# A four-layer transformer kernel: VectorE's work of the linear attention in other gaps, the up projections begun in another order, and the last attention's turns taken earlier

## The reference, cut to what matters

```python
# layer 2, one direction (the other one runs over the flipped tokens)
decay = exp(where(mask, b[:, :, :, None] - b[:, :, None], -inf))   # b = cumsum(loga)
attn = einsum('bhid,bhjd,bhijd->bhij', q, k, decay)
o = attn @ v + einsum('bhid,bhde->bhie', q * exp(b), S)
o = rms(o_forward + flip(o_backward)) * g_gla * silu(r)
# layer 3, per query block of 128
q = apply_rope(rms_norm(h @ w_q, g_q)); k = apply_rope(rms_norm(h @ w_k, g_k))
o = softmax(q @ k.T * 128 ** -0.5) @ v
# every layer, behind its mixer
h = norm(h + gate * (o @ w_out)); y = act(modulate(h) @ w_up) @ w_down
```

## Time and profile before

| | us |
|---|---|
| median of 3 runs (lowest to highest) | 4195.52 (4193.74 to 4201.62) |
| profiled execution, its own time | 4201.74 |
| its span | 4199.9 |
| TensorE busy | 4017.6 (96%) |
| VectorE busy | 1745.0 (42%) |
| ScalarE busy | 830.5 (20%) |
| GpSimd busy | 292.7 (7%) |
| mean granted clock of TensorE | 0.984 |

### The profile page before, as it was taken

The page is one execution under the profiler, slowest core; times in us unless marked ns, Lnnn a source line. Parts: engine busy times, 40 slices in busy tenths (PEclk is TensorE's granted clock), DMA queues, the critical chain, the costliest instruction groups (busy, mean ns, idle before and its releaser), DMA issues.

```text
span 4199.9 us, 46273 instructions
## 1 busy us (share of the span) xinstructions
PE 4017.6 (96%) x18592; PEld 2493.8 (59%) x18592; DVE 1745.0 (42%) x3018; ACT 830.5 (20%) x1643; POOL 292.7 (7%) x396
## 2 busy tenths in 40 slices
PE   7999999999999999999999997799999999999999
PEld 6676588744455555458745645645555444658864
DVE  0254523101257566444202016637786014437841
ACT  1266111100122222211102014421100021531000
POOL 1000000000003422400000002200000000000000
PEclk9999999999999999999999998999999999999999
DMA  5255011211112222312313112401111111002222
GB/s 182 92 200 183 20 61 60 72 60 40 44 61 91 71 81 90 121 56 88 106 62 111 40 40 102 157 26 57 54 60 61 55 67 63 11 21 82 90 91 75
DMA packets 201200, 325.65 MB, mean 78 GB/s; under 512 B 4274, under 2 KB 90632, under 8 KB 200864
## 3 DMA queue, kind: packets, MB, share of 16 engines
q1 hardware_dynamic: 195136, 302.00, 21.2%
q0 software_dynamic: 5856, 20.73, 1.6%
HBM read 320.56 MB, written 2.16 MB: 77 GB/s over the span
## 4 chain that ended last, share of the span: by engine, by line
PE 90%; DVE 5%; ACT 3%; issue 1%; DMA 1%; POOL 0%; DVEq 0%; ACTq 0%
PE PS L992 27%; PE PS L1032 25%; PE PS L967 3%; PE PS L1509 3%; PE PS L945 3%; PE PS L1086 3%; PE PS L1523 3%; PE PS L904 2%; PE PS L821 2%; PE PS L1510 1%; PE PS L1670 1%; PE PS L1200 1%; PE PS L1680 1%; PE PS L1169 1%; PE PS L947 1%
## 5 line engine op out<-in xcount | busy, mean ns | idle before, releaser
L992 PE MATMUL PS<-RING,BIG 128*128 128x512 f32 x2352 | 1016.6, 593 | 3.7 <-DVEq L1737 1.6
L992 PEld LDWEIGHTS PS<-RING,BIG 128*128 128x128 f32 x2352 | 445.5, 190 | 556.8 <-issue 551.9
L1032 PE MATMUL PS<-UT,RING 128*128 128x256 f32 (+1 forms) x2432 | 643.4, 412 | 16.2 <-ACT BIG L2546 15.1
L1032 PEld LDWEIGHTS PS<-UT,RING 128*128 128x128 f32 x2432 | 463.5, 191 | 157.7 <-issue 20.5
L1032 PE MATMUL PS<-BIG,RING 128*128 128x256 f32 (+1 forms) x1824 | 487.8, 410 | 1.8 <-DVEq L1757 1.0
L1823 DVE TENSOR_TENSOR RES_TMP<-PS,GATE 128x512 f32<-128x512 f32 x80 | 55.3, 691 | 1019.7 <-PE PS L992 950.7
L1032 PEld LDWEIGHTS PS<-BIG,RING 128*128 128x128 f32 x1824 | 345.9, 190 | 107.9 <-DVEq L1757 3.1
L2529 ACT ACTIVATE UT<-PS,COL 128x128 f32<-128x128 f32 x328 | 118.8, 467 | 136.2 <-PE PS L882 134.3
L967 PE MATMUL PS<-RING,UT 128*128 128x512 f32 x320 | 139.6, 598 | 2.5 <-ACT BIG L2834 0.9
L992 PE MATMUL PS<-RING,UT 128*128 128x512 f32 x320 | 139.2, 593 | 2.0 <-issue 1.2
L1509 PE MATMUL PS<-UT,RING 128*128 128x512 f32 x256 | 132.4, 599 | 4.4 <-issue 3.7
(11 more groups left out here) (407 smaller groups left out, 4804.0 us busy)
## 6 DMA issues: line engine op xcount, KB each, us to landing
RING<-w_mod_dram SPq DMA_DIRECT2D x48, 2048.0 KB, 8.1
RING<-w_ffn_up_dram SPq DMA_DIRECT2D x44, 1024.0 KB, 5.0
RING<-ff_w_dram SPq DMA_DIRECT2D x32, 1024.0 KB, 5.5
RING<-ff_w_dram SPq DMA_DIRECT2D x16, 2048.0 KB, 8.0
RING<-ssm_w_in_dram SPq DMA_DIRECT2D x8, 2048.0 KB, 8.2
RING<-w_ffn_down_dram SPq DMA_DIRECT2D x8, 1536.0 KB, 6.6
RING<-w_ffn_down_dram SPq DMA_DIRECT2D x8, 1280.0 KB, 5.9
RING<-ssm_w_out_dram SPq DMA_DIRECT2D x4, 2048.0 KB, 8.1
```

Of the source, the lines that this page charges most:

```text
L992: m = mm(bank(t), inp[:, kk, t * 128:(t + 1) * 128], w[:, k, :], start=kk == 0, stop=kk == kn - 1)
L1032: m = mm(bank(bank_, n), a[:, k, :], b[:, k, :], start=k == 0, stop=k == 3)
```

## The change

In layer 2's levels, `heads` is split in two, and both parts move from behind the even step into the next odd step (behind levels 4 and 5). The five `differences` of an even step are spread over the even step before it (two) and the odd step before it (three, behind levels 0 to 2); those of an odd step stand together behind the odd step before it. ScalarE's `level_decays` follow, part 0 of an even step now before the copy of `mod_rows`. For the up projections, the sums of the first weights are made in two halves behind the residuals of the second and third tile from the end, `sums_ready` is posted one instruction earlier, in layers 0 and 1 ScalarE takes the last root and the first product in the middle of the tokens before the last, and in layer 0 also the second first product before the last tokens; there the first token sums come before the last norm and TensorE makes `one(1)` before the last turn. In layer 3 the keys and the first two tiles of queries are turned between the tiles of the second half of the projection, in PSUM banks 4 to 7; the other two tiles are turned inside the attention (steps 3, 4, 6 and 7), and VectorE's last two pieces are scaled and rotated there too (steps 0 to 3).

```diff
-                turn_tokens(L, "f", ntok - 1)
+                if L:
+                    turn_tokens(L, "f", ntok - 1)
                 one(1)
+                if L == 0:
+                    turn_tokens(L, "f", ntok - 1)
                 two(1)
                 for p in range(2):
...
-                by_token(t0 + 2, [8], f, UT, TL)
-                f = flow(3, "turned", 2)
-                stage(f)
-
-                for t in (0, 3):
+                ft = flow(3, "turned", 2)
+                start[ft] = taken.get(ft, 0)
+
+                def keys(t):
+
                     pe.wait_ge(S("L3_heads_normed"), t + 3)
-                    x = place(f) * 1024
+                    x = 2048 + place(ft) * 1024
                     for h in range(2):
                         for j in range(3):
                             m = tr(PS[:, x + h * 384 + j * 128:x + h * 384 + (j + 1) * 128], B_QK[:, t + j, 1024 + h * 128:1024 + (h + 1) * 128], ident)
-                    m.then_inc(f.full, 1)
-                for t in range(TL):
+                    m.then_inc(ft.full, 1)
+
+                def queries(t):
+
                     pe.wait_ge(S("L3_heads_normed"), NT + TL + t + 1)
-                    x = place(f) * 1024
+                    x = 2048 + place(ft) * 1024
                     for h in range(8):
                         m = tr(PS[:, x + h * 128:x + (h + 1) * 128], B_QK[:, t, h * 128:(h + 1) * 128], ident)
-                    m.then_inc(f.full, 1)
-                attend(3)
+                    m.then_inc(ft.full, 1)
...
+                def half_of_queries(t, half):
+
+                    pe.wait_ge(S("L3_heads_normed"), NT + half * TL + t + 1)
+                    pe.wait_ge(ft.free, taken[ft] + ft.slots)
+                    place(ft)
+                    for h in range(4):
+                        m = tr(bank(7, 128, h * 128), B_QK[:, t, half * 512 + h * 128:half * 512 + (h + 1) * 128], ident)
+                    m.then_inc(ft.full, 1)
+
+                w = ring(weights(t0 + 2))
+                for t in range(TL):
+                    place(f)
+                    for k in range(KD):
+                        m = mm(bank(t), UT[:, k, t * 128:(t + 1) * 128], w[:, k, :], start=k == 0, stop=k == KD - 1)
+                    if t < TL - 1:
+                        m.then_inc(f.full, 1)
+                    else:
+                        used(m)
+                    if t < 2:
+                        keys(3 * t)
+                    else:
+                        queries(t - 2)
+
+                def between(step):
+
+                    if step == 1:
+                        pe.wait_ge(ft.free, taken[ft] + ft.slots)
+                    if step in (3, 4):
+                        half_of_queries(2, step - 3)
+                    if step in (6, 7):
+                        half_of_queries(3, step - 6)
+
+                attend(3, between)
+                settled.append(ft)
 
...
                     modulation(next_of[L])
                 for t in range(ntok):
-                    if which == "m" and t == ntok - 1:
-                        sums_of_weights(L, 0)
                     added(1, t)
+                    if which == "m" and t in (ntok - 3, ntok - 2):
+                        half_of_sums_of_weights(L, 0, t - ntok + 3)
+                    if which == "m" and L == 0 and t == ntok - 1:
+                        sums_of_tokens(L, 0)
...
+                        if dr == 1 and v_ < 3 and n + 1 < 2 * NT:
+                            differences(n + 1, [4 + v_])
                         if v_ == 3 and n + 1 < 2 * NT:
                             products(n + 1, 0)
-                        if v_ in (4, 5) and n + 2 < 2 * NT:
+                        if dr == 0 and v_ in (4, 5) and n + 2 < 2 * NT:
                             differences(n + 2, [v_ - 2])
+                        if dr == 1 and v_ == 4 and t:
+                            heads_scaled(t - 1)
+                        if dr == 1 and v_ == 5 and t:
+                            heads_gated(t - 1)
                     post("L2_attention_ready")
                     if n + 1 < 2 * NT:
                         products(n + 1, 1)
-                    if n + 2 < 2 * NT:
-                        differences(n + 2, range(4, 7))
-                    if dr == 0 and t:
-                        heads(t - 1)
-                heads(NT - 1)
+                    if dr == 1 and n + 2 < 2 * NT:
+                        differences(n + 2, range(2, 7))
+                heads_scaled(NT - 1)
+                heads_gated(NT - 1)
 
...
-                attend(3)
+
+                last = len(head_pieces()) - 1
+                for s_ in range(last - 1):
+                    squares(s_)
+                    scaled(s_)
+                    rotated(s_)
+                squares(last - 1)
+                squares(last)
+
+                def between(k):
+
+                    if k in (0, 2):
+                        scaled(last - 1 + k // 2)
+                    if k in (1, 3):
+                        rotated(last - 1 + k // 2)
+
+                attend(3, between)
...
 
-            def sums_of_weights(L, p):
+            def half_of_sums_of_weights(L, p, part):
 
                 t = T0[L, "up"] + p
                 dve.wait_ge(wfull[t % 2], 16 * (t // 2 + 1))
                 a11, a12, a21, a22 = weight_blocks(t % 2)
                 s1, s2, s3, s4 = weight_sums(t % 2)
-                step.go(V.tensor_tensor(s3, a11, a21, ALU.subtract))
-                step(V.tensor_tensor(s1, a21, a22, ALU.add))
-                step(V.tensor_tensor(s2, s1, a11, ALU.subtract))
-                step(V.tensor_tensor(s4, a12, s2, ALU.subtract))
+                if part == 0:
+                    step.go(V.tensor_tensor(s3, a11, a21, ALU.subtract))
+                    step(V.tensor_tensor(s1, a21, a22, ALU.add))
...
+
+            def sums_of_weights(L, p):
+
+                half_of_sums_of_weights(L, p, 0)
+                half_of_sums_of_weights(L, p, 1)
+
+            def sums_of_tokens(L, t):
+
+                half = half_tiles(L)
+                n = 128 * half
+                lo, hi = slice(0, 4), slice(4, 8)
+                t2, t3, t4 = token_sums(L)
+                f, freed = turned[L, "f", t + half]
+                dve.wait_ge(f.free, freed)
+                x = slice(t * 128, t * 128 + 128)
+                y = slice(n + t * 128, n + t * 128 + 128)
+                step(V.tensor_tensor(t3[:, :, x], UT[:, hi, y], UT[:, lo, y], ALU.subtract))
+                step(V.tensor_tensor(UT[:, lo, y], UT[:, lo, y], UT[:, lo, x], ALU.subtract))
+                step(V.tensor_tensor(t2[:, :, x], UT[:, hi, y], UT[:, lo, y], ALU.subtract))
+                if t == half - 1:
+                    post("sums_ready")
+                step(V.tensor_tensor(t4[:, :, x], UT[:, hi, x], t2[:, :, x], ALU.subtract))
...
-            def turned_tokens(L, which, t, b=6):
+            def turned_tokens(L, which, t, b=6, between=None):
 
                 f = flow(L, "tokens_turned", 1)
                 p = int(t >= TL)
                 w = 2 * (which == "f")
                 ready(f)
                 for k in range(KD):
+                    if k == KD - 4 and between:
+                        between()
...
+                elif L < 2 and which == "m":
+
+                    def last_root_and_first_product():
+                        root(L, which, ntok - 1)
+                        first_product(L, 0)
+
+                    for t in range(ntok - 1):
+                        if t:
+                            turned_(t - 1)
+                        root(L, which, t)
+                    turned_tokens(N, w, ntok - 2, between=last_root_and_first_product)
+                    if L == 0:
+                        first_product(L, 1)
+                    turned_(ntok - 1)
...
+                    if dr == 1 and n + 1 < 2 * NT:
+                        level_decays(n + 1, 1)
+                    if dr == 0 and n + 2 < 2 * NT:
+                        level_decays(n + 2, 0)
                     if 2 in next_of:
                         mod_rows(3, n, 7, MOD_ROWS[2])
-                    if n + 2 < 2 * NT:
+                    if dr == 1 and n + 2 < 2 * NT:
                         level_decays(n + 2, 0)
                     if dr == 1 and t:
                         turned(t - 1)
-                    if n + 2 < 2 * NT:
+                    if dr == 1 and n + 2 < 2 * NT:
                         level_decays(n + 2, 1)
                     if dr == 1:
...
                         give(q, A(B_QK[:, t, c0:c0 + 512], bank(t), ACT.Copy))
                     post("L3_qk_in")
-                    if s_:
+                    if s_ and c0 != 512:
                         root_of(s_ - 1)
+                    if c0 == 512:
+                        ready(ft)
+                        x = 2048 + t % 2 * 1024
+                        if t < 2:
```

(24 more changed lines are left out.)

59 lines of the change are left out of this document (33 added, 26 removed).

## The result

The changed kernel takes 4167.53 us, the median of 4 runs (4166.24 to 4168.65), against 4196.91 us for the kernel before on the same chip (4 runs, 4193.74 to 4201.62). The ratio is 0.9927, 95% interval 0.9912 to 0.9942: 29.4 us less, where the sum of the prediction was 29.2.

What follows compares the result with a forecast made beforehand. TensorE, with 90% of the chain that ended last, was taken as the bound, so gains lie only in its waits. Linear attention 12, up projections 8.9 and layer 3's attention 8.3 sum to 29.2 us: 4195.5 to 4166, range 4155 to 4180.

Steps and rivals of the forecast that it cites:

- Linear attention, 12: Layer 2's linear attention: 2.5 us in each of four middle rounds, 1 each in first and last; 12 us, bounds 4 and 18.
- I take them as gained, bounds 0 and 1.5: Linear attention's odd step: the 1.5 us of TensorE's matmuls at a lower rate behind its wait would be won back.
- a sign of being wrong: Signs named: mod_columns waits over 3 us, the granted clock falls in the new waits too, or first five heads over 20 us.
- The lower bound of 4: Linear attention's least gain, 4 us, if the lower clock is kept and nothing is hidden.
- heads, "about 1.9": Linear attention: heads takes about 1.9 of VectorE's 3.40 us behind the even step, and leaves that place.
- Up projection, 4.3, 4.0, 0 and 0.6: Gains in us in the up projections of layers 0, 1, 2 and 3, together 8.9 us.
- Layer 3's attention, 8.3: Scores start 11.9 us earlier, 2.0 and 1.4 are paid back; 8.3 us taken, bounds 4 and 10.
- (a): Linear attention: ScalarE's copy of mod_rows is not late, four times 1.3 us more, 4161 us; chance 0.10.
- (b): Linear attention: ScalarE's wait is long, mod_rows slips by 3 us, levels give 5 instead of 12, 4173 us; chance 0.10.
- (c): Layer 3's first heads: VectorE becomes the bound, the moved 7.8 us come back, gain there 4, 4170 us; chance 0.13.
- (d): All stages: the waits only move, time within 8 us of 4195; chance 0.04.
- (e): Linear attention: TensorE waits at mod_columns in five odd steps; slower from 5.8 us each, 4206 us at 8; chance 0.03.

Runs made afterwards that it cites:

- rows_first: The changed kernel with ScalarE copying mod_rows before part 0 of level_decays in the even step too; linear attention 7.0 us less than in the changed kernel.
- both: The changed kernel with mod_rows copied ahead of part 0 and the last piece but one scaled and rotated before the attention; 4161.7 us, ratio 0.9911 to the kernel before.
- gla_only: The kernel before with the linear attention's part of the change alone; 0.26% faster, 10.9 us of 4200.
- att_only: The kernel before with the part in layer 3's attention alone; 0.22% faster, 9.2 us of 4200.
- pieces_first: The changed kernel with VectorE's work on the last two pieces all ahead of layer 3's attention; 3.8 us longer than the changed kernel in the profiled stage.
- after_again: The changed kernel, unaltered, timed once more beside its three parts; 4172.0 us, 0.65% faster than the kernel before.
- up_only: The kernel before with the up projections' part of the change alone; 0.20% faster, 8.4 us of 4200.
- one_piece: The changed kernel with VectorE's last piece but one scaled and rotated before layer 3's attention; 0.85 us gained in the profiled stage.
- sums_back: The changed kernel with the four sums of weights back ahead of the last residual; 2.2 us more in layers 0 and 1 each, median 9.0 us above the changed kernel's second timing.

## Why the prediction was right, by its steps

The total, 29.2 us, met 29.4 by the first comparison and 27.3 by the second, and the three parts agree one by one. The terms inside them are less good than the total.

- **Linear attention, 12.** Measured 11.7 in the profile, 10.9 in the time. The first and last rounds gave 1.8 and 1.0 (forecast 1 and 1), the middle ones 8.8 (10). The level 7 wait went from 4.72 to 1.05 us (1.4), the new wait is 1.29 (1.1), the output comes 2.2 us earlier per round (2.5). What failed is the step "I take them as gained, bounds 0 and 1.5": in three of the four rounds the clock still fell, now behind the new wait. The prediction had named just that as a sign of being wrong. The part still met because these rounds came only 1.2 us short together and the first round gave 0.8 more than forecast. So ScalarE's late copy was mis-sized, at 1.1 us of waiting a round, or 1.5 with the differences; rows_first shows 1.8 for it, and both 1.5. The lower bound of 4 doesn't follow either: with the clock kept low and nothing hidden, its own terms leave nothing of the 2.5 us per round, and about 1 in all.
- **heads, "about 1.9".** The prediction gave its move no price of its own. In one profile it is more than half of the part, 6.4 of 11.7 us, since with heads in the old place the wait is 2.98 us and the clock stands at 0.89 and not 0.93. 2.2 of it are in the last round.
- **Up projection, 4.3, 4.0, 0 and 0.6.** Measured 4.2, 3.9, about 0 and 0.4. The 1.2 us for the slow product of layer 1 hold only against the execution shown: in gla_only and att_only that product waits 3.12 us too, takes 1.97 us, and the stretch is 14.5 and not 15.6. Against such an execution the part gives 2.9 there. In layer 3 the 0.4 is less than what the clock does: att_only took 12.8 us with the old code, the changed code 12.4 to 14.1.
- **Layer 3's attention, 8.3.** Scores come 12.3 us earlier (11.9), and 3.9 are paid back (3.6): 8.4. The shares are other than forecast. The first five steps take back 2.9 us and not 2.0. One of VectorE's moved pieces costs 0.85 us of the 3.9; how the rest divides between the other piece, the table load and the half turns wasn't measured, since the clock hid it in pieces_first. The 1.7 us behind the attention were in no term.
- **Rivals.** (a), the copy of `mod_rows` not late, didn't happen, but rows_first makes it happen by an edit: 7 us, where (a) had 5.2. (b) had a wait 3 us longer; it is 1.3. (c) gave the attention 4: it gave 8.4. (d) and (e) are out: in each of the three stages the gain stayed and did not merely turn into another wait, and `mod_columns` waits in four odd steps, the longest 1.3 us where (e) needed 5.8.

The table load in the row at 2610.71 takes 1.28 us, the next activation starts at 2612.00, and part 0 with its load takes 4.66 us in all:

```profile
2612.00 1.06 ACT L2891 ACTIVATE UT<-UT 128x1024 f32<-128x1024 f32 x1
```

By the Trainium skill (ScalarE: Activation LUTs, What ACT_TABLE_LOAD costs) a change of table set takes 2.66 us, about 1.28 of it the load and the rest a drain. By an estimate from that figure the new wait would be 2.7 us. The trace agrees on the load, but it has no drain behind it, and the wait is 1.29.

## What to carry to other kernels

When a move takes a wait out of TensorE's way, look at once for the next, shorter wait on the same chain, here another engine's copy that the reordering itself had made late. A wait of 1 to 3 us in front of TensorE has a price beyond its length if the granted clock falls behind it, so the last such wait in a loop can be worth more than the first. And before a stage's gain is read off two single traces, compare a stage that the diff leaves alone: here it differed by 7.9 us, about what one part was worth. In the same way, before a round is taken as typical, look at its neighbours: here one of four ran without the fall of the clock.

## What the runs showed of the hardware

The granted clock isn't the same in two executions of one code. Two stretches of layer 1's mixer, which is the same in all these kernels and starts within 1.5 us of the same time in these three. First the changed kernel's first profile:

```profile
1136.00:1180.00 44.00, 38.72 (x148) 21.34 (x146) 16.97 (x28) 7.54 (x19) 6.05 (x9) 0.96 0.46 142
1420.00:1440.00 20.00, 19.25 (x258) 12.48 (x250) 15.27 (x16) 8.78 (x14) 16.55 (x13) 1.00 0.36 124
```

The same code in after_again:

```profile
1136.00:1180.00 44.00, 38.32 (x127) 20.07 (x126) 16.27 (x27) 7.55 (x19) 5.76 (x9) 0.88 0.45 141
1420.00:1440.00 20.00, 19.25 (x257) 12.20 (x251) 15.27 (x16) 8.51 (x13) 16.61 (x13) 1.00 0.41 133
```

And up_only:

```profile
1136.00:1180.00 44.00, 38.43 (x128) 20.05 (x127) 16.48 (x27) 7.55 (x19) 5.98 (x9) 0.88 0.45 141
1420.00:1440.00 20.00, 18.49 (x187) 11.26 (x184) 13.24 (x14) 7.73 (x13) 13.60 (x12) 0.91 0.40 133
```

From the first turn of tokens before it (1105.74 in the first of these profiles) to its output projection that mixer took 630.5 us in the changed kernel's first profile and 634.4 in its second, 638.4 in the kernel before, and from 633.5 to 644.6 in the other kernels. Hence the 7.9 us of that stage between the profiles before and after: the execution of the changed kernel that was profiled first had the shortest of all, and the span of the second is 4169.6 us where the first has 4164.8. It is also the likeliest reason that runs of unchanged code spread over 10 us and more (4193.4 to 4207.2 in 27 runs): the mean granted clock of the six fastest of these is 0.986 to 0.988, of the six slowest 0.982 or 0.983. So 5 rounds couldn't tell one_piece from the changed kernel.

Equal waits don't fix it either. Behind 3.1 us of waiting the product two(0) of layer 1's up projection took 2.96 us in the kernel before and 1.97 in gla_only, att_only and sums_back; in layer 0 it was slow in all four. What decides between the two stays open.
